# The RWKV scan of a fused transformer kernel: b and k joined into one 128-wide stationary operand, updates contracted over 128 rows

## The reference, cut to what matters

```python
def step(s, inp):
    rt, wt, kt, vt, at, bt = inp
    sa = jnp.einsum('bhij,bhj->bhi', s, at)
    s = s * wt[:, :, None, :] + sa[..., None] * bt[:, :, None, :] + vt[..., None] * kt[:, :, None, :]
    y = jnp.einsum('bhij,bhj->bhi', s, rt) if with_out else None
```

## Time and profile before

| what | before |
|---|---|
| median of 3 runs | 3533.31 us (3530.44 to 3544.45) |
| the profiled execution, its own time | 3544.86 us |
| its span, first to last instruction | 3543.0 us |
| mean granted TensorE clock | 0.966 |
| PE busy over the span | 3212.4 us (91%) |
| DVE, ACT, POOL busy | 1534.2, 1148.9, 404.1 us |
| the scan's stretch | 1494 to 2178 us, 684 us |

### The profile page before, as it was taken

How to read it: one execution, slowest core, us unless ns; L and a number is a source line. 1 busy time by engine, 2 the same in 40 slices (tenths; PEclk the granted TensorE clock), 3 DMA queues, 4 the chain that set the end, 5 groups by cost and what they waited for, 6 DMA issues and landing times. The chain is left out here.

```text
span 3543.0 us, 84567 instructions
## 1 busy us (share of the span) xinstructions
PE 3212.4 (91%) x38814; PEld 2573.9 (73%) x38814; DVE 1534.2 (43%) x2633; ACT 1148.9 (32%) x2233; POOL 404.1 (11%) x512
## 2 busy tenths in 40 slices
PE   7998998999999889888888889999989997999998
PEld 5766976799999848777777776899977775534343
DVE  3354446433233363266666663434435554111112
ACT  3343233322122332355555553322343333000001
POOL 0000013100000210133323320000012101000000
PEclk8999999999999999999999999999999998799999
DMA  4394144111111211000000002222121124499996
GB/s 186 115 363 163 48 184 167 72 72 72 48 72 67 73 48 48 8 6 6 6 13 30 7 4 97 95 96 96 72 70 48 66 92 172 198 428 410 412 424 285
DMA packets 35284, 437.81 MB, mean 124 GB/s; under 512 B 5040, under 2 KB 5648, under 8 KB 9200
## 3 DMA queue, kind: packets, MB, share of 16 engines
q1 hardware_dynamic: 29856, 414.10, 29.5%
q0 software_dynamic: 5072, 18.30, 1.6%
HBM read 425.56 MB, written 6.82 MB: 122 GB/s over the span
## 5 line engine op out<-in xcount | busy, mean ns | idle before, releaser
L755 PE MATMUL ps<-part 128*128 128x512 f32 (+1 forms) x4656 | 857.2, 346 | 41.8 <-DVE part L998 15.5
L755 PEld LDWEIGHTS ps<-part 128*128 128x128 f32 x4656 | 734.6, 194 | 160.6 <-issue 18.5
L2057 PE MATMUL ps<-part 128*128 128x256 f32 x1856 | 515.9, 278 | 3.3 <-DVE part L2098 3.3
L2058 PE MATMUL ps<-part 128*128 128x256 f32 x1856 | 515.7, 278 | 0.0
L2059 PE MATMUL ps<-part 128*128 128x256 f32 x1856 | 515.7, 278 | 0.0
L4012 PE MATMUL ps<-part 128*64 128x512 f32 x1536 | 374.9, 608 | 28.8 <-DMA part<-in_wg 14.1
L2098 DVE TENSOR_TENSOR part<-part 128x1024 fp32r<-128x1024 f32 x128 | 158.1, 1235 | 488.3 <-ACT part L2087 488.3
L2557 PE MATMUL ps<-part 64*64 64x64 f32 x9984 | 308.6, 222 | 57.2 <-issue 45.0
L2057 PEld LDWEIGHTS ps<-part 128*128 128x128 f32 x1856 | 348.8, 188 | 4.0 <-ACT part L2161 3.8
L2058 PEld LDWEIGHTS ps<-part 128*128 128x128 f32 x1856 | 350.9, 189 | 0.2
L2059 PEld LDWEIGHTS ps<-part 128*128 128x128 f32 x1856 | 348.4, 188 | 0.0
(11 more groups left out here) (429 smaller groups left out, 5021.0 us busy)
## 6 DMA issues: line engine op xcount, KB each, us to landing
part<-in_ada_w SPq DMA_DIRECT2D x36, 2048.0 KB, 9.1
part<-in_mlp_w SPq DMA_DIRECT2D x32, 2048.0 KB, 7.8
part<-in_wg SPq DMA_DIRECT2D x32, 2048.0 KB, 14.6
part<-in_wu SPq DMA_DIRECT2D x32, 2048.0 KB, 13.1
part<-in_wd SPq DMA_DIRECT2D x32, 2048.0 KB, 13.9
part<-in_b_in SPq DMA_DIRECT2D x8, 2048.0 KB, 7.7
part<-in_ab_w_in SPq DMA_DIRECT2D x7, 2048.0 KB, 7.9
part<-in_rkv SPq DMA_DIRECT2D x6, 2048.0 KB, 7.6
```

Of the source, the lines that this page charges most:

```text
L755: mm = pe.e.matmul(ps[:, j * n:j * n + n], lhs, rhs, start=k == ks[0] and i == 0, stop=k == ks[-1] and i == 2)
L2057: pe.e.matmul(ps, wh[:, k, :], hi[:, k, x], start=k == 0, stop=False)
L2058: pe.e.matmul(ps, wh[:, k, :], lo[:, k, x], start=False, stop=False)
```

## The change

The change rewrites the stages of the scan on all engines:

- b and k of a chunk and head stand side by side in one tile `bs` (576 columns), so that a 64-row, 128-column operand `u.pair(hd, g)` holds both. `bk` is 16 matmuls with that as stationary and the identity as moving operand. `keys` takes the place of `ka` and `br`: 16 matmuls with the same stationary and [a, r] as moving operand (128 columns; 64 in the context), masked by four DVE operations where three stood.
- V and the solutions U stand on opposite partition halves of one tile `r.V[:, x, hd, :]`. `outputs` and `states` contract over 128 rows, 4 matmuls of 128x64 each, where 8 of 64x64 stood; the identity x Z of `states` is one 128x128 matmul of 128 columns.
- The second level of the inverse is left out of it: `XMT` and `XM` 2 go, and the stream gets a stage: `t` (X times RH, copied to T by ACT), `mt` (M2 times T), and DVE adds T and `mt` into V's free half, in two operations.
- `squares 1` and `X add` 0 share a stationary: 16 matmuls of 128 columns, and 16 `squares turned`, where 48 stood.
- The product with A_k is started early, as a step of its own (`av`), and so is the r Z part of the outputs (`yz`). Their banks are taken there.
- In `turned`, the matmuls whose output is on half 0 become `pe.transpose`.
- On POOL the product for b is two operations per direction, one per head half, behind a DVE operation (`bb`).
- All six tables have new numbers.

The diff, cut to its core:

```diff
+    r.NX = nx.rearrange("p (b c) -> p b c", c=64)
+    r.NP = nx[:, 0:1024].rearrange("p (d x g c) -> p d x g c", d=2, x=2, g=4)
+    r.X = [K.shaped(nx[:, o:o + 512], 2, 4, 64) for o in (1024, 1536, 2048)]
+    r.G = [[K.alloc(2, 4, 128)]]
+    r.BK = [K.flat(1024).rearrange("p (h d g c) -> p h d g c", h=2, d=2, g=4) for _ in range(2)]
...
-CROSSED_AT = {"gram": 12.06, "X turned": 22.53, ("PX", 1): 23.08, ("XM", 1): 25.44, ("PX", 2): 27.45, ("XM", 2): 29.2,
-              **stream_at("rh", 31.91), **stream_at("uu", 32.91), **stream_at("out", 34.11)}
-STRAIGHT_AT = {"squares 0": 13.61, ("X add", 0): 15.5, "squares 1": 16.4, ("X add", 1): 17.77, "squares 2": 19.06,
-               ("X add", 2): 20.57, "bk": 22.59, "ka": 23.84, "XMT": 24.39, "br": 26.58, **stream_at("zz", 34.08),
-               "v turned": 2.27}
...
+CROSSED_AT = {"gram": 12.488, "X turned": 21.324, ("PX", 1): 24.197, ("XM", 1): 26.479, ("PX", 2): 29.482,
+              **stream_at("rh", 29.367), **stream_at("t", 29.708), ("v turned", 1): 7.01, ("v turned", 0): 30.518,
+              **stream_at("yz", 30.519), **stream_at("out", 31.967)}
+STRAIGHT_AT = {"squares 0": 14.349, "squares 1": 17.211, ("X add", 1): 18.741, "squares 2": 18.974, ("X add", 2): 20.344,
+               **stream_at("mt", 30.437), **stream_at("av", 27.536), "keys": 23.227, "bk": 20.844, **stream_at("zz", 31.78)}
+WHOLE_AT = {"lora": 0, "norms": -5.692, "y centred": 49.919, "y var": 51.412, "coef": 55.94, "gates": 57.252}
...
+    def pair(self, hd, g):
+
+        at = 2 * self.toks[g // 2][g % 2].start + 64 * hd
+        return self.bs[half(hd), at:at + 128]
...
+                if hd ^ flip:
+                    mm = pe.e.matmul(out, block[h, :], K.ident[h, h], start=True, stop=True)
+                else:
+                    mm = pe.e.transpose(out, block[h, :], K.ident[h, h])
...
+    def values(n, sub):
 
         bank = K.bank("rh", n, sub)
+        first = n % 3 == 0 and sub == 0
         for u in both(K, n):
             g, cs, x = u.chunk(sub)
-            first = u.b == 0 and sub == 0
-            ps = bank[:, 64 * u.d:64 * u.d + 64]
-            pe.wait_ge(K.at("A", u.d, n), K.at("v rows", u.m))
+            pe.wait_ge(K.at("A", u.d, n), K.at("v rows", u.m, int(u.b == 0)))
+            for hd in range(2):
+                o = half(1 - hd)
+                mm = pe.e.matmul(bank[o, 64 * u.d:64 * u.d + 64], u.G[o, hd, g, 0:64], r.V[o, x, hd, :], start=u.d == 0,
+                                 stop=first, skip_group_check=True)
+            if u.d:
+                mm.then_inc(*pe.up(("rh", n, sub) if first else ("av", n, sub)))
...
+    def last_level(n, sub):
+
+        pe.wait_ge(K.at("t in", n, sub), K.at("M", n, 2))
+        bank = K.bank("mt", n, sub)
+        for u in both(K, n):
+            g = u.chunk(sub)[0]
+            for hd, o in halves():
+                mm = pe.e.matmul(bank[o, 64 * u.d:64 * u.d + 64], u.M2[o, g, :], r.T[o, u.d, :], start=True, stop=True)
...
+            for hd in range(2):
+                mm = pe.e.matmul(bank[half(1 - hd), 64 * u.d:64 * u.d + 64], r.V[:, x, hd, :], u.G[:, hd, g, 64:128],
+                                 start=False, stop=True, skip_group_check=True)
+            if u.d:
+                mm.then_inc(*pe.up(("y", n, sub), *streamed(n, sub)))
...
+        if not first:
+            pe.wait_ge(K.at("zm", n, sub))
+            pe.e.matmul(bank[:, 0:128], K.ident, r.zm[sub % 2].rearrange("p d c -> p (d c)"), start=True, stop=False,
+                        skip_group_check=True)
...
+                mm = pe.e.matmul(ps[o], u.BK[:, hd, g, :], r.V[:, x, hd, :], start=first, stop=True, skip_group_check=True)
...
+        if step == "squares 1":
+            pe.wait_ge(K.at("NP", n, 1), K.at("X", n, 0))
+            for u in both(K, n):
+                ps = K.bank(("squares", 1), *u.key)
+                for g in range(4):
+                    i, j = 8 * u.d + g, 16 + 8 * (n % 3) + 4 * u.d + g
+                    for hd, h in halves():
+                        mm = pe.e.matmul(ps[h, 128 * g:128 * g + 128], u.NP[h, 1, g, :], r.NX[h, i:j + 1:j - i, :],
+                                         start=True, stop=True)
+                    if g == 3:
+                        mm.then_inc(*pe.up((("squares", 1), *u.key)))
+                    yield
+            ps = K.bank("squares turned", n)
+            for u in both(K, n):
+                yield from blocks(ps, 256 * u.d, u.NP[:, 0], u.NP[:, 1], 0, *([("squares turned", n)] if u.d else []))
...
+            banks = [K.bank("bk", n, hd) for hd in range(2)]
             for u in both(K, n):
                 pe.wait_ge(K.at("made", *u.key))
-                ps = K.bank("bk", *u.key)
-                for i, w in enumerate((u.bb, u.ks)):
-                    yield from turned(ps, 256 * i, [w[:, u.toks[it][j]] for it in range(2) for j in range(2)], 0,
-                                      *([("bk", *u.key)] if i else []))
-        if step == "ka":
+                for g in range(4):
+                    for hd, o in halves():
+                        mm = pe.e.matmul(banks[hd][:, 256 * u.d + 64 * g:256 * u.d + 64 * g + 64], u.pair(hd, g), K.ident[o, o],
+                                         start=True, stop=True)
...
+        if step == "keys":
             for u in both(K, n):
                 pe.wait_ge(K.at("made", *u.key))
-                ps = K.bank("ka", *u.key).rearrange("p (g x c) -> p g x c", g=4, x=2)
-                to = slice(0, 4, 3) if u.lat else slice(0, 1)
-                yield from gram(ps[:, :, 0:2 if u.lat else 1, :], u, u.ks, u.ops[:, to, :], 0, ("ka", *u.key))
-        if step == "br":
-            pe.wait_ge(*[K.at("made", d, n) for d in range(2)])
-            ps = K.bank("br", n).rearrange("p (d g x c) -> p d g x c", d=2, g=4, x=1)
-            for u in both(K, n):
-                yield from gram(ps[:, u.d], u, u.bb, u.ops[:, 3:4, :], 0, *([("br", n)] if u.d else []))
-        if step == "v turned":
-            for j, (x0, x1) in enumerate(BOTH):
-                ps = K.bank("v turned", n // 3, j)
-                yield from turned(ps, 0, [a.vT[:, n // 3, x:x + 64] for x in range(x0, x1, 64)], 0, ("v turned", n // 3, j))
+                banks = [K.bank("keys", *u.key, hd).rearrange("p (g x c) -> p g x c", g=4, x=2) for hd in range(2)]
+                w = 2 if u.lat else 1
+                for g in range(4):
+                    for hd, o in halves():
+                        mm = pe.e.matmul(banks[hd][:, g, 0:w], u.pair(hd, g), u.ar[o, 0:w, u.toks[g // 2][g % 2]], start=True,
+                                         stop=True)
...
+        if step[0] == "mt":
+            yield from last_level(n, step[1])
...
+        if step == ("X add", 0):
+            for u in both(K, n):
+                sums = K.ps.of(("squares", 1), *u.key).rearrange("p (g x c) -> p g x c", g=4, x=2)
+                v.wait_ge(v.now(), K.at("NP from", *u.key))
+                v.e.tensor_tensor(u.X, u.X, sums[:, :, 1, :], ADD).then_inc(
+                    *v.up(("X", n, 1), free(("squares", 1), *u.key)))
...
+            x0, x1 = (u.chunk(sub)[2] for u in both(K, n))
+            xs, turn = slice(min(x0, x1), max(x0, x1) + 1, abs(x1 - x0)), slice(None, None, 1 if x0 < x1 else -1)
+            sums = K.ps.of("mt", n, sub)[:, 0:128].rearrange("p (d c) -> p d c", d=2)
+            for hd, o in halves():
+                v.e.tensor_tensor(r.V[o, xs, hd, :], r.T[o, turn, :], sums[o, turn, :], ADD).then_inc(
+                    *v.up(("uu in", n, sub), free("mt", n, sub)))
...
+            s.e.activation(r.T.rearrange("p d c -> p (d c)"), K.ps.of("t", n, sub)[:, 0:128], ACT.Copy).then_inc(
+                *s.up(("t in", n, sub), free("t", n, sub)))
...
+                pool.e.tensor_tensor(u.ks, fours[2], fours[1], MUL).then_inc(*pool.up(("made", *u.key)))
+                pool.wait_ge(K.at("kk av", *u.key))
+                for hd, o in halves():
+                    pool.wait_ge(pool.now())
+                    pool.e.tensor_tensor(u.bb[hd], fours[0][o], fours[1][o], MUL).then_inc(
+                        *pool.up(("made", *u.key), ("tmp used", *u.key)))
```

More of the change, by code:

```diff
@@ new lines @@
+DVE_AT = {"B": 2.55, "B mid": 5.441, "B before": 5.686, "aa": 12.1, "bb": 9.334, "gram": 13.085, "X": 14.117,
+          ("X add", 0): 18.669, ("X add", 1): 19.409, ("X add", 2): 21.665, ("M", 1): 25.004, ("XM", 1): 28.839,
+          ("M", 2): 30.302, "kk sum": -5.105, "kk": 7.699, "gate rest": 49.335, "y scaled": 55.243, "rw y": 57.666,
+          **stream_at("zz", 32.004), **stream_at("mt", 30.984), "keys": 24.264}
+POOL_AT = {"gain": 3.806, "kr": 5.803, "bb": 8.194, "rr": 12.823, "k dir": 1.536}
@@ L2540, in rw_pe, with gram @@
     a, pe, r = K.a1, K.pe, K.rw
[L2542 to L2551, removed]
+    def gram(out, u, turn, *done):
+        for g in range(4):
+            t = u.toks[g // 2][g % 2]
+            for hd, o in halves():
+                two = u.aa[o, t], u.bb[hd][:, t.start // 64]
```

(31 more changed lines are left out.)

244 lines of the change are left out of this document (121 added, 123 removed).

## The result

The changed kernel takes 3734.2 us (median of 4 runs, 3730.1 to 3743.5) where the kernel before takes 3531.9 beside it (4 runs, 3523.8 to 3544.5): ratio 1.058, interval 1.0563 to 1.0597. It is slower by 202 us; the prediction said 3529, with a range up to 3600.

A forecast was written before the change was run, and what follows sets the result against it. It took instruction supply to PE as the scan's bound before. After: array 610, waits 37, ramps 13, starvation 20, so 680 us against 684, minus 4; forecast 3529 us, range 3450 to 3600.

The forecast's parts named there:

- count of array time: PE's work in the scan, priced by tile shape and changes of shape: 496 us before, 610 us after the change.
- transposes -6: Term of the array time after: 288 of the 64x64 products become transposes, leaving one record instead of two, 6 us less.
- starvation: PE in the scan waiting for instructions where four quadrants run for long: bounded between 0 and 60 us, taken as 20.
- array work with its ramps: PE's array time in the scan after the change, 610 us, and 13 us left to ramps.
- The other waits: PE's real waits in the scan, not for instructions: 37 us, taken to stay as before.
- Instruction supply as the bound of the kernel before: In the scan, packets of about 256 instructions come 3.75 us apart: 634 us of supply against 496 us of array time.
- the 37 packets: Sign: some 37 fewer instruction packets in the scan, 132 instead of 169, coming over 4.5 us apart on average.
- The price of 64x128: A matmul pair of 64x128 (`bk`, `keys`) takes 52 ns a record, 0.21 us a pair, whatever it moves; the wide load binds.
- rival 2: Slower: PE meets `zz` or `out` before DVE's additions are done, 0.4 us at each of 96 subs: 3567 us, chance 0.18.
- the ends named: Starvation 0 or 60 (-20, +40), 128x64 pairs at 0.215 (+32), change of shape at 0.21 (+22): 3495 to 3570.
- 1: Rival, faster: the scan's 64x64 pairs share as often as before (76%) and starvation goes entirely: 3461 us, chance 0.27.
- 3: Rival, slower: PE's "issue" gaps (83.5 us) belong to the scan's stretches, not instruction supply, and stay: 3593 us, chance 0.10.

The follow-up runs named there:

- experiment 1: The changed kernel with both products of each pair in `turned` written as matmuls, no transposes in the scan: 3542.3 us, ratio 1.0032 to the kernel before.
- experiment 3: The kernel before, with only the matmul and transpose alternation added in `X turned` and `v turned` (288 transposes): 3604.0 us, ratio 1.0205 to the kernel before.
- experiment 4: The changed kernel with matmuls in `X turned` and transposes left in `v turned` alone (96 of the 288): 3578.4 us, ratio 1.0127 to the kernel before.

## Why the prediction was wrong

**The step that failed** is in the count of array time: "288 of the 64x64 are transposes", and then "transposes -6". I took them as pairs with one record less. They are 576 changes between two kinds of work, each 0.15 to 0.17 us from start to start, and they cost 192 us in the end instead of -6, about half of it through the clock. The prediction had the price: it gave 0.17 us for a change of shape and named the rule of the Trainium skill (TensorEngine Tiling (Array Packing), Key Properties) that a change of tiling mode drains TensorE, but applied it to shapes alone. The earlier trace rows showed only transposes in a row, where no switch is to be seen, and no row showed one between matmuls; both ends of that unknown should have stood in the range. At 0.17 us they would have given 576 x 0.17 = 98 us, 3633 in all: the right side, out of the range, and still 101 us short of the 3734 measured.

**The second gap** is the clock. Every price was at full clock, since the scan before ran at 0.98, and the range had no case in which it falls. It is about half of the loss.

**The rest of the sum held.** Without the transposes (the -6 given back) the prediction is 3535 us, measured 3542. The scan: 686 against 681. That it comes so close is in part luck, since two errors cancel: starvation was put at 20 us, and the issue gaps are 2.4 (1.5 and 0.9), while array work with its ramps, put at 610 + 6 + 13 = 629, shows as 643 us of busy time. The other waits were put at 37 us and are 36. Instruction supply as the bound of the kernel before: right, by the gaps (83.5 us, and 2.4 in experiment 1), the 37 packets and experiment 3. The Trainium skill's sentence that fetch is mostly hidden (Runtime: NRT & Kernel Launch, Instruction fetch mechanics) fits the changed kernel and not the one before. The price of 64x128 held too: 768 records of `bk` in 48.7 us, 63 ns each with their entries, where 52 without them had been read. Two slips changed nothing in the sum. The text gives 0.17 us for a wait for the state's DVE operation, where 4.3 / 13 is the 0.33 that rival 2 uses. And the ends named do not add up to 3495 to 3570: the low one is -20, the high ones together +94 (3623), which is still far below 3734.

**DVE**: 472 us predicted, 430 measured, 435 in experiment 1. The additions cost what was said (192 x 0.285 = 55 us), but three others became shorter (below). Busy time in the scan: ACT +11 of +12, POOL +24 of +38.

**The rivals.** 1 (better packing, 3461): not seen even in experiment 1, where PE is busy for 643 us in a scan of 681. 2 and 3: ruled out by the waits above. A fourth, "transposes among matmuls drain", was missing. Of the signs named, issue gaps under 40 us, PE busy over 620 and 37 packets came true although the forecast failed: they tell that the supply was freed, not what took its place.

## What to carry to other kernels

Count each alternation between kinds of work on TensorE (matmul and transpose, one tile shape and another) at some 0.15 us, on each side, in the order that is left once the steps of all tables are merged, and do not alternate inside an inner loop: a pair by plain matmuls with the identity took 0.12 us together with its neighbour's pair, where with the "cheaper" transpose the two took 0.44. Then look at the granted clock: here its fall doubled the bill. Where the profile shows "issue" gaps, fewer instructions do help, but only by as much as the array's own time leaves.

## What the runs showed of the hardware

- Changes of tile shape go with the same fall of the clock as transposes do: 0.86 with transposes, 0.84 with 64x32 tiles between 64x64, 1.00 with neither. The low stretches of the changed kernel last 3 to 10 us, most of them 10, and come about once per unit (36 us).
- The 542 changes of shape in the rest of the scan left the clock at 1.00 in experiment 1, and rows of 16 switches in 3.1 us left it at 1.00 right behind them in experiment 4. It fell where such rows stood behind `bk`'s 64x128 tiles; whether that is the reason was not tested.
- Three DVE operations on two operands in SBUF, at the same shape 128x256, took 814, 546 and 593 ns a piece before (steps `B before`, `aa`, `bb`) and 418, 528 and 479 in experiment 1. `B before`, whose operation is the same in both kernels, first before, then in experiment 1:

```profile
L2892 DVE SCALAR_TENSOR_TENSOR part<-part 128x256 f32<-128x256 f32 x48 | 37.2, 814 | 0.0
```

```profile
L2950 DVE SCALAR_TENSOR_TENSOR part<-part 128x256 f32<-128x256 f32 x46 | 17.3, 418 | 0.0
```

What slowed it before, POOL at work at the same time or something else, was not tested.
